# Two-block transformer kernel: an opening ordered by token tile 0, the output projection's weights in two query blocks' places, eight row slots from the first rows

## The reference, cut to what matters

```python
ret = head_rmsnorm(o_rf + flip_seq(o_rb)) * jax.nn.silu(rg)   # bidir_mix
gla = head_rmsnorm(o_gf + flip_seq(o_gb)) * jax.nn.silu(gg)
y = jnp.concatenate([ret, gla], axis=-1)
x = x + g1 * (y.astype(x.dtype) @ w_out)                       # trunk_layer
x = x + g2 * peer_ffn(modulate(rmsnorm(x, norm2_w), sh2, sc2), peer_w_q, ...)

def block(xb):                                                 # 128 tokens, in peer_ffn
    q = (xb @ w_q).astype(F32).reshape(PEER_BLOCK, PEER_HEADS, 2, half)
    s1 = jnp.einsum("thd,hnd->thn", q[:, :, 0], k1.astype(F32))
    s2 = jnp.einsum("thd,hnd->thn", q[:, :, 1], k2.astype(F32))
    ...                                   # top 16 of the sums of both top 16
    u = down[idx]                         # 16 rows a head and token
    act = jax.nn.gelu(jnp.einsum("thkd,td->thk", u, xb).astype(F32), approximate=False)
    return jnp.einsum("thk,thkd->td", (g * act).astype(xb.dtype), up[idx])
```

## Time and profile before

| what | value |
|---|---|
| profiled execution | 3155.42 us, span 3153.9 us |
| median of the runs | 3158.4 us |
| PE, DVE, ACT, POOL busy | 82%, 64%, 39%, 34% of the span |
| DMA moved | 1179.94 MB, of which the gathers 1073.81 MB |
| last "go" product ends, opening begins | 359.1 us |
| first row's gather is issued | 428.00 us |

### The profile page before, as it was taken

One profiled execution on the slowest core, in us unless ns is written; L12 is line 12 of the kernel. 1 busy time (PEld: TensorE's weight loads), 2 busy tenths in 40 slices (PEclk: granted clock), 3 DMA queues, 4 the chain that ended last, 5 costly groups with the idle time before them and its releaser, 6 DMA issues.

```text
span 3153.9 us, 35978 instructions
## 1 busy us (share of the span) xinstructions
PE 2590.0 (82%) x12092; PEld 1062.2 (34%) x12092; DVE 2022.2 (64%) x5008; ACT 1228.9 (39%) x3892; POOL 1059.6 (34%) x1041
## 2 busy tenths in 40 slices
PE   7999998878777877778888888888777877978777
PEld 3555653323222323223333353323223332322111
DVE  4533457777777777665555757677777776765544
ACT  3122335443443444334223534444344443443323
POOL 0000014433434334333333333344344443433431
PEclk9999999999999999999999999999999999999999
DMA  9311359999999999999999999999999999999995
GB/s 370 140 54 54 133 200 411 421 421 416 414 421 420 419 409 421 421 417 410 420 412 421 420 422 419 416 419 415 417 415 416 416 419 419 404 420 421 421 421 241
DMA packets 161020, 1179.94 MB, mean 374 GB/s; under 512 B 20994, under 2 KB 21700, under 8 KB 24004
## 3 DMA queue, kind: packets, MB, share of 16 engines
q0 software_dynamic: 147456, 1073.81, 82.4%
q1 hardware_dynamic: 13380, 103.84, 8.2%
HBM read 1175.48 MB, written 2.10 MB: 373 GB/s over the span
## 4 chain that ended last, share of the span: by engine, by line
DMA 46%; PE 16%; ACT 5%; DVE 4%; issue 3%; POOL 2%; DVEq 0%; POOLq 0%
DMA ring<-in_expert_rows,idx_v 16%; DMA scr<-in_expert_rows,idx_v 11%; DMA ring<-in_peer_rows,idx_v 10%; PE banks L1163 9%; DMA scr<-in_peer_rows,idx_v 9%; PE banks L811 7%; DVE ring L2296 2%; DVE scr L2296 1%; POOL ring L785 1%; POOL scr L785 1%; ACT ring L1685 1%; ACT L1679 1%; ACT scr L1679 1%; ACT L1641 1%; ACT ring L1667 0%
## 5 line engine op out<-in xcount | busy, mean ns | idle before, releaser
L1163 PE MATMUL banks<-ring 128*32 128x512 f32 x2016 | 816.8, 623 | 267.2 <-ACT ring L1685 257.4
L1163 PE MATMUL banks<-scr,ring 128*32 128x512 f32 x2080 | 820.6, 620 | 206.1 <-ACT ring L1685 205.6
L1679 ACT ACTIVATE scr<-scr 128x1 f32<-128x1 f32 x1024 | 206.9, 202 | 1503.3 <-DVE scr L2296 1502.0
L2296 DVE CUSTOM_DVE_ANT_0 ring<-ring 128x1024 f32<-128x1024 f32 x378 | 463.1, 1225 | 315.0 <-DMA ring<-in_expert_rows,idx_v 167.5
L2296 DVE CUSTOM_DVE_ANT_0 scr<-scr,ring 128x1024 f32<-128x1024 f32 x390 | 477.8, 1225 | 292.0 <-DMA scr<-in_peer_rows,idx_v 147.2
L785 POOL DMA_INDIRECT scr<-in_peer_rows,idx_v x264 | 273.0, 1034 | 481.3 <-PE banks L1163 363.5
L1163 PEld LDWEIGHTS banks<-ring 128*32 128x32 f32 x2016 | 163.7, 112 | 786.9 <-ACT ring L1685 503.5
L1163 PEld LDWEIGHTS banks<-scr,ring 128*32 128x32 f32 x2080 | 166.9, 111 | 728.3 <-ACT ring L1685 446.1
L785 POOL DMA_INDIRECT ring<-in_expert_rows,idx_v x256 | 261.5, 1022 | 432.3 <-PE banks L1163 399.5
L811 PE MATMUL banks<-hT,scr 128*128 128x128 f32 (+3 forms) x2576 | 364.0, 301 | 48.9 <-DVE ring L2278 47.3
L785 POOL DMA_INDIRECT ring<-in_peer_rows,idx_v x248 | 259.2, 1045 | 403.2 <-PE banks L1163 364.4
(11 more groups left out here) (255 smaller groups left out, 2245.9 us busy)
## 6 DMA issues: line engine op xcount, KB each, us to landing
scr<-in_w_in SPq DMA_DIRECT2D x8, 2048.0 KB, 11.7
scr<-in_w_mod SPq DMA_DIRECT2D x7, 2048.0 KB, 12.2
ring<-in_w_in SPq DMA_DIRECT2D x7, 2048.0 KB, 12.3
scr<-in_w_q SPq DMA_DIRECT2D x6, 2048.0 KB, 11.8
ring<-in_w_mod SPq DMA_DIRECT2D x5, 2048.0 KB, 12.3
scr<-in_peer_w_q SPq DMA_DIRECT2D x4, 2048.0 KB, 12.6
scr<-in_peer_rows,idx_v POOLq DMA_INDIRECT x264, 15.8
ring<-in_w_out SPq DMA_DIRECT2D x2, 2048.0 KB, 7.7
```

Source lines behind the costliest of these rows:

```text
L1163: last = nc.tensor.matmul(psum[2 + c][32 * g:32 * g + 32, :], spread[:, i % 8, :], rows[slot_of(i)][:, D + c * CW:D + (c + 1) * CW], start ...
L1679: nc.scalar.activation(gelu[:, h, k:k + 1], dots[:, h, k:k + 1], ACT.Gelu if i < N_ROWS else ACT.Gelu_apprx_tanh).then_inc(gelu_done, 1)
L2296: V.tensor_tensor_reduce(u, u, xq[g], 1.0, 0.0, ALU.mult, ALU.add, dots[:, n % 2, k:k + 1]).then_inc(dotted, 1)
```

## The change

1. The weights of the second mixer's gates are loaded early into place 0, and its gates ("gg") are computed where those of the first ("rg") were, in between the steps of the second mixer. "rg" now comes in the opening, a tile at a time; ACT applies silu in the bank, DVE multiplies from it (`gate_ret`).
2. `yT` is made by tile (t, half), not by column block: tile 0 first.
3. `w_out` is loaded behind "go" into blocks 1 and 2. Query block 3 gets `peer_w_q`'s part 1 behind `y_done`; parts 2 and 3 go into blocks 1 and 2 when the halves of "wo" have been computed.
4. `slot_of` turns over all eight slots from row 0. Slots 0 and 1 wait for "gg", 2 and 3 for "rg", 6 and 7 for the last `yT`.
5. Heads 4 to 31 begin their search 8 rows later; the parts of "wo", the norms of tiles 1 to 3 and a few loads move with it.

```diff
-    if i < 4:
-        return 4 + i
-    if i < OPENING:
-        return (4, 5, 6, 7, 0, 1)[(i - 4) % 6]
-    return (2, 3, 0, 1, 4, 5, 6, 7)[(i - OPENING) % SLOTS]
+    return (4, 5, 0, 1, 2, 3, 6, 7)[i % SLOTS]
...
-        return 12 * n - 16
+        return 12 * n - (16 if n < 4 else 8)
...
             full(sp, "go", TT - 1, 1)
+            for n in range(2):
+                sp.dma_start(block[1 + n], a["w_out"][n].rearrange("p (k n) -> p k n", n=CW)).then_inc(w_out_in[n], 16)
             load_block(0, w_q_rows, 0)
             sp.dma_start(kT, a["peer_keys"]).then_inc(keys_in, 16)
-            load_block(1, w_q_rows, 1)
-            load_block(2, w_q_rows, 2)
-            full(sp, "yT", KT - 1)
-            load_block(3, w_q_rows, 3)
+            sp.wait_ge(y_done, TT)
+            load_block(3, w_q_rows, 1)
+            for n in range(2):
+                full(sp, "wo", TT - 1, n)
+                load_block(1 + n, w_q_rows, 2 + n)
...
-                elif slot < 4:
-                    full(pool, "wo", TT - 1, slot // 2)
+                elif slot in (0, 1):
+                    full(pool, "gg", TT - 1)
+                elif slot in (2, 3):
+                    full(pool, "rg", TT - 1)
+                elif slot in (6, 7):
+                    full(pool, "yT", TT - 1, 1)
...
+            def turn_heads(t):
+
+                pe.wait_ge(y_done, 1 + t)
+                empty(pe, "rg", t)
+                for half, src in ((0, o_ret), (1, o_gla)):
+                    o = begin("yT", t, half)
+                    for h in range(HEADS):
+                        last = nc.tensor.transpose(o[:, h * P:(h + 1) * P], src[:, t, h * P:(h + 1) * P], ident)
+                    last.then_inc(bank_ready, 1)
...
+                ret_gate_part(1, 0, 4)
                 tile_rows("n1", 0)
+                ret_gate_part(1, 4, 6)
                 all_empty(pe, "nt", "n1", 0, 1)
                 scores_q(0)
                 scores_s(0)
-                project("wo", 2, w, (0,))
+                ret_gate_part(1, 6, KT)
+                ret_gate_part(2, 0, KT)
                 quad_rows(0, 0, 0)
+                quad_rows(0, 1, 2)
+                ret_gate_part(3, 0, 2)
                 move_idx(0)
...
+                move_gate(0)
+                ret_gate_part(3, 2, KT)
+                for t in (1, 2, 3):
+                    turn_heads(t)
+                add_pair(0)
+                empty(pe, "rg", 3)
                 scores_q(1)
                 scores_s(1)
-                add_batch(0)
-                project("wo", 3, w, (0,))
+                add_pair(1)
+                empty(pe, "yT", 3, 0)
+                empty(pe, "yT", 3, 1)
+                project_part("wo", 1, w, 0, 0)
                 add_pair(2)
```

More of the change, by code:

```diff
@@ L40 @@
 SLOTS = 8
-OPENING = 38
 N_HEADS = TT * PH
@@ L340, in plan_jobs @@
             jobs.add(("go", c, odd), "A")
-    for t in range(TT):
-        jobs.add(("gg", t), "A")
-    for k in range(KT):
-        jobs.add(("yT", k), alternate(k))
+    jobs.add(("rg", 0), "D")
+    for half in range(2):
+        jobs.add(("yT", 0, half), "AD"[half])
     for n in range(2):
@@ L347, in plan_jobs @@
     tile("n1", 0, (0, 1))
+    for t, bank in ((1, 6), (2, 7), (3, 5)):
+        jobs.add(("rg", t), "D", bank)
+    for t in (1, 2, 3):
+        for half in range(2):
+            jobs.add(("yT", t, half), "AD"[half], 6 + half)
     for t, n, bank in LAST_HALVES:
@@ L1078, in _, with ret_gate_part @@
                     from_scores(c, h, BWD).then_inc(bank_ready, 1)
-            w = use_chunk("w_in", W_GG)
-            to_rows([("gg", t) for t in range(TT)], hT, w, TT)
-            for k in range(KT):
-                o = begin("yT", k)
-                pe.wait_ge(y_done, 1 if k < HEADS else 1 + TT)
-                src = o_ret if k < HEADS else o_gla
-                for t in range(TT):
-                    last = nc.tensor.transpose(o[:, t * P:(t + 1) * P], src[:, t, (k % HEADS) * P:(k % HEADS + 1) * P], ident)
-                last.then_inc(bank_ready, 1)
+            w_rg = use_chunk("w_in", W_RG)
+            def ret_gate_part(t, first, last):
+                o = psum[jobs.bank[jobs.number("rg", t)]]
+                if first == 0:
+                    opened("rg", t)
+                if last == KT:
+                    begin("rg", t)
+                for k in range(first, last):
+                    ins = mm(o[:, :], hT[:, k, t * P:(t + 1) * P], w_rg[:, k, :], k, KT)
+                if last == KT:
+                    ins.then_inc(bank_ready, 1)
+            def turn_heads(t):
[6 more added lines that the diff above has]
+                    last.then_inc(bank_ready, 1)
+            ret_gate_part(0, 0, KT)
+            turn_heads(0)
             def project(name, t, w, halves=(0, 1)):
@@ L1226, in sums, with project_part @@
                         beside[p]()
-            def project_part(name, t, w, part):
-                o = begin(name, t, 1) if part == 0 else psum[jobs.bank[jobs.number(name, t, 1)]]
+            def project_part(name, t, w, part, n=1):
+                o = begin(name, t, n) if part == 0 else psum[jobs.bank[jobs.number(name, t, n)]]
                 for k in range(KT // 2 * part, KT // 2 * (part + 1)):
-                    last = mm(o[:, :], yT[:, k, t * P:(t + 1) * P], w[1][:, k, :], k, KT)
+                    last = mm(o[:, :], yT[:, k, t * P:(t + 1) * P], w[n][:, k, :], k, KT)
                 if part == 1:
@@ L1240, in start_first @@
             def start_first():
[L1242 to L1248 removed]
+                w = [block[1 + n] for n in range(2)]
+                empty(pe, "yT", 0, 0)
+                empty(pe, "yT", 0, 1)
+                for n in range(2):
+                    pe.wait_ge(w_out_in[n], 16)
+                    project("wo", 0, w, (n,))
+                ret_gate_part(1, 0, 4)
                 tile_rows("n1", 0)
+                ret_gate_part(1, 4, 6)
                 all_empty(pe, "nt", "n1", 0, 1)
@@ L1435, in _ @@
                       472: lambda: products(2), 489: lambda: products(TT - 1)}
-            for t, first in ((2, 8), (3, 13)):
+            for t, first in ((1, 9), (2, 12), (3, 15)):
                 beside[first] = lambda t=t: project_part("wo", t, w, 0)
-                beside[first + 2] = lambda t=t: project_part("wo", t, w, 1)
+                beside[first + 1] = lambda t=t: project_part("wo", t, w, 1)
             for t in range(2):
@@ L1728, in start_first @@
                 quads_out(0, 2, 2)
+                ret_silu(3)
                 gated_e32(0)
+                for t in (1, 2, 3):
+                    heads_out(t)
                 pairs(0, 1, {})
@@ L2524, in _ @@
                       959: lambda: tile_mean("fin", 2), 963: lambda: final(2)}
-            for t in (1, 2, 3):
-                beside[13 + 8 * t] = lambda t=t: tile_mean("n1", t)
-                beside[17 + 8 * t] = lambda t=t: tile_rstd("n1", t)
+            for t, first in ((1, 31), (2, 43), (3, 59)):
+                beside[first] = lambda t=t: tile_mean("n1", t)
+                beside[first + 4] = lambda t=t: tile_rstd("n1", t)
             for j in range(4):
```

148 lines of the change are left out of this document (75 added, 73 removed).

## The result

The changed kernel took 3169.07 us (median of 6 runs, 3164.13 to 3171.25) against 3158.13 us before (6 runs, 3156.47 to 3160.3): a ratio of 1.0033, interval 1.0022 to 1.0044. The forecast was 3157 us, with a range of 3149 to 3167. The profiled execution took 3164.13 us (a span of 3162.7), 8.7 us over the one of before.

A forecast was written before the change was run, and what follows sets the result against it. DMA row gathers bound the kernel once full, PE the opening before that. Start -16.0, holes +4.4 and late blocks +10.0 sum to -1.6 us: 3156.8, said as 3157 us, range 3149 to 3167.

The forecast's parts named there:

- Part 1: Way to the first gather: it goes out at 412.0, 16.0 us earlier, not 21.9, as PE's queue delays the index move.
- Rival D: Loads of w_out share the engines with the keys, tile 0's projection starts at 378: +7.4, 3166 us; chance 0.05.
- Part 3: Two late peer_w_q blocks, 4.19 MB, pass when the DMA engines are full and delay the rows behind: +10.0 us.
- a hole near row 40: Sign of being wrong: a DMA hole near row 40 or 64, pointing to C, or Part 2 and Part 4.
- Part 4: Heads 4 to 31 ending their search 8 rows later: costs nothing; if it shows, one hole of 1 to 2 us.
- Part 2: Opening with eight slots, first gather to full DMA engines: latency and holes 17.3 us against 12.9, +4.4.
- Scaled to the 115 us of the new list ... I take off 3.7.: Opening's holes: 3.7 us off 21.0 for overlapping neighbouring pairs, calibrated on 5 us found in the kernel before.
- The list: PE's work and waits in written order through the opening: pair 0 ends at 431.4, pair 7 at 486.5.
- Row 21 ... has landed at 487.8.: End of the opening's account: row 21, issued 480.9, landed 75.8 us after the first gather, 54.8 of them transfer.
- C: Slower by holes at pairs 0 to 7, each waiting 1.3 us more: holes 27.7, +8.8, 3167 us; chance 0.19.
- B: PE has no holes of its own, opening waits overlap with other work: holes 8.2, -10.7, 3147.7 us; chance 0.22.

The follow-up runs named there:

- e2: Kernel before, with only parts 2 and 3 of peer_w_q loaded late, after 8 and 24 summed rows: 3167.49 us, 1.0034 over before.
- e1: Changed kernel, its two late peer_w_q loads cut to one eighth of each block, so other experts are chosen: 3156.36 us, 0.9993 over before.
- e8: Changed kernel with the searches of heads 4 to 31 begun at 12 n - 16 again, as before: 3161.19 us, 1.0019 over before.
- e5: Changed kernel unaltered, measured and profiled again: 3161.09 us, 1.0014 over the kernel before.
- e9: Changed kernel unaltered, in the third measurement on another chip: 3161.36 us, 1.0015 over the kernel before.
- e11: Repeat of e3 (changed kernel, six half parts of the output projection moved behind pair 7), third measurement: 3155.08 us, 0.9998 over before.
- e4: Changed kernel with six row slots instead of eight for rows 0 to 37: 3168.50 us, 1.0036 over the kernel before.
- e6: e3 with six row slots instead of eight for rows 0 to 37: 3161.24 us, 1.0017 over the kernel before.
- e12: Repeat of e6 (later half parts, six slots for rows 0 to 37) in the third measurement: 3159.17 us, 1.0014 over before.
- e10: Repeat of e4 (changed kernel, six slots for rows 0 to 37) in the third measurement: 3165.56 us, 1.0031 over before.
- e7: e3 with dot products 2 to 7 and pairs 1 to 3 put ahead of head 1's search and head 2's queries: 3145.34 us, 0.9968 over before.
- e3: Changed kernel with six later half parts of the output projection moved behind pair 7: 3154.64 us, 0.9991 over the kernel before.

## Why the prediction was wrong

**Part 1, the first gather: right.** Forecast 412.0 with go at 359.11, so 52.9 us after it; the three profiles of the changed kernel have 52.5, 52.5 and 54.0 (410.14, 409.48 and 414.21 less go). That the index move would stand behind twelve gate steps and two quads held, and with it the 16.0 us instead of 21.9. `w_out` was there: PE's gate steps start at 357.42 and tile 0's projection at 367.79, 10.4 us later, as forecast (358.9 to 369.3). Rival D is out.

**Part 3, the late weights: right for the kernel before.** 10.0 forecast, 10.3 in e2. In the changed kernel the full 10 isn't shown (e1: 7.9 by the medians and 5.2 at row 60 of the profile, for 8.7 left out). The issues came at some 489.6 and 541.8 instead of 484 and 529. The prediction's sign of being wrong, "a hole near row 40", came too, and is the second of these loads: in the changed kernel's timeline of DVE row 40 waits 4.32 us for DMA,

```profile
551.16 1.23 DVE L2341 CUSTOM_DVE_ANT_0 scr<-scr,ring 128x1024 f32<-128x1024 f32 x1 [4.32 <-DMA scr<-in_peer_rows,idx_v]
```

though its DMA engines are full there (a share of 1.01 from 530 to 580), and in e1, without that load, the row waits for nothing. The Trainium skill's 358 GB/s ("DMA: Bandwidth & Descriptors", Bandwidth) would have said 11.7 for the two blocks. But the same section gives that figure for both cores of a memory domain streaming, and 425 GB/s for 16 MB on a core alone; the 420 GB/s in the slices of this one core agree with the latter.

**Part 4: right** (e8, +0.1 us).

**Part 2, the holes between row 0 and full engines: the step that failed.** The forecast was 17.3 us of latency and holes, 4.4 over the 12.9 of before. Counted in the same way to row 22, which is the last one that PE holds up (time from the first gather less 23 x 2.49, less 5.0 for the block that lands in it): 12.9 before, 23.8 in e5, 24.0 in e9, 29.6 in the first profile. So the term was 6.5 us too small in the undisturbed profiles, and 12.3 in the first. With the measured terms the sum closes: for e5 -16.4 + 10.9 + 10.0 = +4.5, and 5.1 from go to row 1023; for the first profile -16.4 + 16.7 + 10.0 = +10.3, and 10.2. This is bookkeeping more than a test. Up to row 22 it must close, as the holes are what is left over there, with the block taken at its full 5.0 (e1 shows 2.4 of them at that row); what it tests is that behind row 22 only the second block is lost.

Where the 6.5 us lie, in the prediction's own words:
- "Scaled to the 115 us of the new list ... I take off 3.7." The list itself was right: it put the end of pair 7 at 486.5, 74.5 us after the first gather, and e5 and e9 both have 75.3. The overlap found in the kernel before doesn't carry over: in e5 it saves 0.43 us at each of pairs 4, 5 and 7 (1.92 for 2.35), and pair 0 loses 1.3 (3.65). The calibration was also read off by 0.9: pair 7 of the kernel before ends at 484.50 by PE's own row, not at 485.4. By the Trainium skill ("TensorE: Matmul & The Clock Gate", Part 3, packing small matmuls) every pair would be at 1.9; in e5 this holds for pairs 4, 5 and 7, not for pairs 1, 3 and 6, which come out of a wait for ACT (2.35), and not for pair 2 (2.75, no wait shown). Cost of this step: 3.7, and 0.8 for the list.
- "Row 21 ... has landed at 487.8." The account ended one pair too early. Row 22 is released by pair 7 and finds empty engines: in the undisturbed profiles it lands some 10.5 us later, 5.0 of them the block in front of it, the rest a lone row's 5.6. This hole, about 2.1 us by my own list (492.4 against 490.3), wasn't counted.

Together 6.6. Without the 3.7 and the 2.1 the forecast would have been -1.6 + 5.8 = +4.2, and the repeated measurements gave +5.7 and +5.9, both inside the stated range (from 9 us under the kernel before to 9 over it). That the two steps make up the term is worked out afterwards; that halves of the projection in this stretch cost 6.3 us was tried (e11).

The other 6 us of the first profile are two things that I did not have. PE stood or crept from 412 to 416: its two quads take 7.6 us to the next instruction, where e5's take 3.5, 4.1 us more. And the clock fell at pair 3 (0.72 from 460 to 464), which took 3.35 us for the 2.35 of the list and of e5 and e9; pair 4 is 1.7 us further behind e5 than pair 3 was. This too is no matter of the stall, as pair 3 takes 3.3 us in e4 and e8 as well. Pair 0 ran slow as well (3.77), but so it did in e5 (3.65) and e9 (3.55), so this 1.3 belongs to the 6.5 above. Stretches of the changed kernel, of the stall and of pair 0:

```profile
412.00:416.00 4.00, 1.78 (x27) 0.83 (x29) 0.00 (x0) 0.00 (x0) 2.35 (x3) 1.00 1.00 350
...
424.00:428.00 4.00, 1.66 (x12) 1.41 (x12) 3.25 (x7) 1.24 (x3) 1.77 (x1) 0.95 0.88 299
428.00:432.00 4.00, 2.46 (x9) 1.24 (x9) 2.79 (x5) 2.82 (x6) 1.90 (x2) 0.50 0.78 256
```

The granted clock is 0.50 in the last, the lower of the two levels (1.2 GHz), after PE had been busy for 1.66 of the 4 us before it. The kernel before had 1.00 from 390 to 530. The lower clock is no matter of the first profile alone: pair 0 takes 3.5 to 3.8 us in eight of the twelve profiles with the new opening, and 2.26 in four (e4, e6, e8, e12), by no rule that I could find.

**The rivals.** C was the one that came: slower by holes, "in pairs 0 to 7, where each sum is queued behind DVE's copies, a search and ACT's table changes", with its test, pair 7 later than about 491 (491.46), and its price, +8.8 (+8.7). That the numbers fit so well is luck: they fit the one profile with the stall, which C didn't have. By the repeated profiles pair 7 is only 0.8 us later after the first gather than my list put it, and the change is slower all the same. B had it the wrong way round: it took the waits for overlapped. That the eight slots are used, which the forecast took for granted, is right: they are worth 4.2 us (e10), 5.0 by my way of counting.

**Where the gain went.** The change brings the first gather forward by 16.4 us, and 10.0 us of weights now pass when the engines are full. What was left, 6.4 us, had to survive the way from row 0 to row 22, and did not: PE had half projections in front of the sums and DVE waited for them (e11: 6.3 us), and dot products of rows that had landed stood behind searches (e7's last dot product comes 8 to 10 us earlier after go than e3's and e11's). Both are matters of order, with the same work, and with both mended the kernel is 10.0 us under the one before. How much of that is the early start isn't shown: the kernel before, with its own halves and searches put in that order, was not run.

## What to carry to other kernels

An earlier start is worth only what is left when the bound resource is full for good, so forecast the time of the last item that still waits for another engine (here row 22), not of the first that starts, and follow each engine's written order up to there, that of the consumer too. Bytes moved from an idle stretch into a full one cost up to their full transfer time (10.3 us for 10.0 in e2, less by e1 in the changed kernel, where the first of them falls into the opening): subtract that first. And before a few us in one profile are explained, count from a common event behind the unchanged part, and profile the same kernel twice.

## What the runs showed of the hardware

- PE can be held up with no wait in the trace: 4 us of pieces of five or six records (about three products) with 0.33 us between them, "issue" as the only reason, from 411.9, while the DMA share rises from 0.03 (408 to 412) to 1.00 (412 to 416) with the first gathers. In the other profiles of the same kernel gathers start at the same place and nothing is held up. That the two are linked was not tried, and that it is the supply of instructions that fails, as the expectations of e5 and e9 call it, is a guess.
- The launch and the attention vary by 4.6 us between executions of the same program up to there (go at 356.13 to 360.70 us). The 2.77 ms behind them repeated within 1.5 us for four kernels with two profiles each; with the stall the changed kernel was 5 us off.
- The ratio of the changed kernel to the one before was 1.0033, 1.0014 and 1.0015 in three measurements, with intervals of 0.001 on either side: the first does not agree with the others as well as its interval says.
